# A hybrid SSD / mLSTM / attention kernel: the cells' gate computed feature-major, and ScalarE's squares behind the decays

## The reference, cut to what matters

```python
h = _f32(_rmsnorm(x, ab_norm_g[i]))
proj = h @ _f32(ab_w_in[i])
z_a, xbc, dt_raw, z_b, q, k, v, ig, fg, og = jnp.split(proj, AB_SPLITS, axis=-1)
# _ssd: the state space part
y = y_diag + y_off + xs * d_skip
y = y.reshape(bsz, seqlen, SSD_INNER) * jax.nn.silu(z)              # z_a
yg = _rms(y.reshape(bsz, seqlen, SSD_GROUPS, SSD_INNER // SSD_GROUPS))
return yg.reshape(bsz, seqlen, SSD_INNER) * norm_g
# _mlstm: the matrix-memory cells
h = num / jnp.maximum(jnp.abs(den), jnp.exp(-m_t))[..., None]
h = h * jax.nn.sigmoid(o_raw)
h = _rms(h).reshape(bsz, seqlen, ML_INNER) * norm_g
return h * jax.nn.silu(z)                                            # z_b, the cells' gate
# after both
y = jnp.concatenate([y_a, y_b], axis=-1) @ _f32(ab_w_out[i])
```

## Time and profile before

| | |
|---|---|
| median of three runs | 1588.63 us (1584.34 to 1589.14) |
| the profiled execution | 1582.52 us, span 1580.6 us |
| PE busy / DVE / ACT / POOL, share of the span | 97% / 58% / 41% / 36% |
| mean granted clock of TensorE | 0.992 of 2.4 GHz |
| projection, 80 to 560 us | PE 40.0 us busy in each 40 us |
| scan, 600 to 720 us | PE 36.9 to 37.2 us busy in each 40 us; DVE 35.8 to 36.4 |

### The profile page before, as it was taken

How to read it: one execution, slowest core, us unless ns; L and a number is a source line. 1 busy time by engine, 2 the same in 40 slices (tenths; PEclk the granted TensorE clock), 3 DMA queues, 4 the chain that set the end, 5 groups by cost and what they waited for, 6 DMA issues and landing times.

```text
span 1580.6 us, 23657 instructions
## 1 busy us (share of the span) xinstructions
PE 1527.5 (97%) x9114; PEld 1313.9 (83%) x9114; DVE 911.6 (58%) x1484; ACT 649.0 (41%) x1272; POOL 567.1 (36%) x325
## 2 busy tenths in 40 slices
PE   9999999999999989998999999999999999999897
PEld 8798989898999977776788877888888888787686
DVE  7675878684853459998544263345544235553623
ACT  6542533353432233444345252344555333556421
POOL 3245454545344346566565430132211113211110
PEclk9999999999999989999999999999999999999999
DMA  5132333342334345755585330022111102103612
GB/s 177 41 127 87 123 92 121 93 130 84 121 120 132 116 138 178 225 168 186 180 291 205 121 120 15 14 68 73 61 54 34 34 15 83 63 35 113 253 67 107
DMA packets 151084, 176.42 MB, mean 112 GB/s; under 512 B 9670, under 2 KB 126658, under 8 KB 149954
## 3 DMA queue, kind: packets, MB, share of 16 engines
q1 hardware_dynamic: 150810, 174.92, 34.0%
q10 hardware_dynamic: 168, 0.06, 0.0%
HBM read 122.46 MB, written 52.43 MB: 111 GB/s over the span
## 4 chain that ended last, share of the span: by engine, by line
PE 47%; DVE 2%; issue 1%; DMA 1%; ACT 0%; POOL 0%; SPq 0%; POOLq 0%; DVEq 0%; ACTq 0%
PE b_ps L2404 22%; PE b_ps L2449 4%; PE b_ps L2424 4%; PE b_ps L2354 3%; PE b_ps L2356 3%; PE b_ps L2355 3%; PE b_ps L2436 2%; PE b_ps L2506 2%; PE b_ps L2507 2%; PE b_ps L2508 2%; PE b_ps L2457 1%; PE b_ps L2372 0%; DMA b_yy<-z 0%; DMA z<-b_y_T 0%; DVE b_y_T L2195 0%
## 5 line engine op out<-in xcount | busy, mean ns | idle before, releaser
L1925 POOL TENSOR_TENSOR b_w<-b_w_raw,b_w 128x1024 fp32r<-128x1024 f32 x66 | 158.3, 2399 | 356.0 <-DVE b_w L2184 252.1
L2404 PE MATMUL b_ps<-a_h_hi,b_w 128*128 128x512 f32 x768 | 264.4, 404 | 2.8 <-DVE a_h_lo L2162 2.8
L393 POOL TENSOR_TENSOR b_w<-b_y_T,b_w 128x1024 fp32r<-128x1024 f32 x54 | 141.0, 2614 | 189.7 <-ACT b_w L451 189.7
L2404 PEld LDWEIGHTS b_ps<-a_h_hi,b_w 128*128 128x128 f32 x768 | 144.4, 188 | 36.8 <-issue 3.9
L2404 PE MATMUL b_ps<-a_h_lo,b_w 128*128 128x512 f32 x384 | 150.0, 391 | 0.0
L941 PE MATMUL b_ps<-b_w,p_hi 128*128 128x256 f32 x768 | 139.2, 283 | 0.0
L700 DVE SCALAR_TENSOR_TENSOR b_w_raw<-p_out_raw,p_cols,b_w_raw 128x1024 f32<-128x1024 f32 x60 | 119.8, 2003 | 12.8 <-ACT b_w_raw L482 11.3
L941 PEld LDWEIGHTS b_ps<-b_w,p_hi 128*128 128x128 f32 x768 | 120.1, 192 | 0.6
L941 PE MATMUL b_ps<-b_w,p_lo 128*128 128x256 f32 x384 | 108.7, 283 | 0.0
L2195 DVE CUSTOM_DVE_ANT_0 b_y_T<-b_ps,a_neg_dist 128x128 f32<-128x128 f32 (+5 forms) x96 | 72.1, 777 | 62.8 <-PE b_ps L2424 52.3
L451 ACT CAST b_w<-b_y_T 128x1024 fp32r<-128x1024 f32 x60 | 62.7, 1045 | 106.3 <-DVE b_y_T L661 54.7
(11 more groups left out here) (417 smaller groups left out, 3562.3 us busy)
## 6 DMA issues: line engine op xcount, KB each, us to landing
b_y_T<-in_ab_w_in SPq DMA_DIRECT2D x33, 512.0 KB, 4.4
tok<-p_out_raw SPq DMA_DIRECT2D x64, 256.0 KB, 2.3
b_w_raw<-in_ab_w_out SPq DMA_DIRECT2D x32, 512.0 KB, 3.7
b_w_raw<-in_c_w_in SPq DMA_DIRECT2D x32, 512.0 KB, 4.1
feat<-b_w_raw SPq DMA_DIRECT2D x20, 512.0 KB, 2.7
c_fe<-feat SPq DMA_DIRECT2D x7, 1280.0 KB, 6.7
yt<-b_y_T SPq DMA_DIRECT2D x8, 1024.0 KB, 10.9
b_y_raw<-yt SPq DMA_DIRECT2D x32, 256.0 KB, 4.0
```

The lines of the kernel that those rows point to most:

```text
L393: gp.tensor_tensor(w_lo[s % SLOTS][:, :, :], operand(n, split_of(n, p))[:, :, :], w_hi[s % SLOTS][:, :, :].bitcast(F32), ALU.subtract).the ...
L1925: gp.tensor_tensor(w_lo[:, w, :], w_raw[u % W_RAW][:, :], w_hi[:, w, :].bitcast(F32), ALU.subtract).then_inc(S["l_wlo"], 1)
L2404: mm = pe.matmul(o, x, y, start=(k == 0 and q == 0), stop=(k == KT - 1 and q == 2))
```

## The change

**In the projection** the two z_b blocks are computed feature-major, by the same matmul form as an f block. ACT multiplies each gated area by the norm's gain (one more instruction for each of the 16 areas, behind a wait for the silu), SP stores them into a new DRAM tensor `zt` (8 x 128 x 1024), and a sixth small load brings the gain. `tok` shrinks to 3072 columns.

**In the scan** the cells' norm (without gate and gain) moves from DVE's L1628 to ACT (`memory_norm`), four instructions; the gate multiplies the turned cells' half in the eviction of `turn(n, 0)`, in place of the gain. The gate is loaded by a transfer of its own (`load_gate_cells`), which SP issues behind the store of y and behind a wait for the eviction of `turn(n, 0)`.

**Orders.** ACT: the third group of decays and the cells' weights come before the fourth group, and the squares of y's state space half behind all of them. DVE: `means` behind `s_st`; `turn(n-1, 1)` ahead of the denominator chain; `low_y(0)` moves from chunk 6 to chunk 7. POOL: the power for the cells' mean stands ahead of y plus skip.

```diff
+    gate_turned = lambda n: kinds[n] == "t" and tok_blocks[number[n]][2] is turned_out
...
+                    if gate_turned(n):
+                        sp.dma_start(dest[c0 + 2 * k + b, :, i * BLK:(i + 1) * BLK], area(i, k, b)).then_inc(stored, 16)
...
+                    if gate_turned(n):
+                        gated[0] += 1
+                        nc.scalar.activation(area(i, k, b), area(i, k, b), func).then_inc(S["silu_z"], 1)
+                        act.wait_ge(S["silu_z"], gated[0])
+                        gain = GAIN + c0 + 2 * k + b
+                        nc.scalar.activation(area(i, k, b), area(i, k, b), ACT.Copy, scale=cols[:, gain:gain + 1]
+                                             ).then_inc(S["a_out"], 1)
...
-                    if kinds[n] == "f":
+                    if kinds[n] == "f" or gate_turned(n):
                         fs = slice(b * P, (b + 1) * P)
...
+def load_gate_cells(sp, chunk, n, into, landed):
+    sp.dma_start(into.rearrange("p (f t) -> p f t", t=P), chunk["zt"][:, :, bass.ds(n * P, P)].rearrange("f p t -> p f t")
+                 ).then_inc(landed, 16)
...
                 sp.wait_ge(S["p_cmem"], n + 1)
-                sp.wait_ge(S["d_yb"], n + 1)
                 sp.wait_ge(S["l_yz"], n + 1)
                 load_chunk(sp, chunk, feat, tok, n + 2, par)
                 if behind_first(n):
                     store_y(n - 1, 1 - par)
+                sp.wait_ge(S["d_yT"], n * 4 + 2)
+                load_gate_cells(sp, chunk, n + 2, gz[par][:, 2, :], in_landed[par])
...
-                pe.wait_ge(S["d_yb"] if part == 0 else S["a_ynorm"], (n + 1) * (part + 1))
+                pe.wait_ge(S["a_yb"] if part == 0 else S["a_ynorm"], (n + 1) * (part + 1))
...
+            def memory_norm(n):
+                act.wait_ge(S["l_rstdm"], n + 1)
+                for h in range(ML_HEADS):
+                    yb = y[:, D + h * ML_V:D + (h + 1) * ML_V]
+                    a = nc.scalar.activation(yb, yb, ACT.Copy, scale=rms[:, 2 + h:3 + h])
+                a.then_inc(S["a_yb"], 1)
...
                 memory_squares(n)
-                if isinstance(n, int) and n == TILES - 2:
-                    high_y(0)
-                decays(n + 1, True)
+                memory_norm(n)
+                decays(n + 1, (0, 1, 2))
+                memory_weights(n + 1)
+                decays(n + 1, (3,))
                 ssd_squares(n)
-                decays(n + 1, False)
-                memory_weights(n + 1)
                 ssd_norm(n)
...
+                gp.wait_ge(S["d_meanm"], n + 1)
+                gp.tensor_tensor(rms[:, 2:6], rms[:, 2:6], half[:, 0:4], ALU.pow).then_inc(S["l_rstdm"], 1)
                 gp.wait_ge(S["d_y"], n * 2 + 2)
                 gp.wait_ge(S["l_xd"], n + 1)
                 gp.tensor_tensor(y[:, 0:D], y[:, 0:D], x_tok[:, :], ALU.add).then_inc(S["l_yd"], 1)
-
-                gp.wait_ge(S["d_meanm"], n + 1)
-                gp.tensor_tensor(rms[:, 2:6], rms[:, 2:6], half[:, 0:4], ALU.pow).then_inc(S["l_rstdm"], 1)
...
                 ssd_weights(0)
-                means()
...
                                          op0=ALU.mult, op1=ALU.mult).then_inc(S["d_st"], 1)
 
+                means()
                 dve.wait_ge(S["l_sdec"], n + 0)
...
+                    by = last(gcols[:, 4 * b:4 * b + 4], P) if part else gate_cells(n, par)[:, 4 * b - 8:4 * b - 4, :]
+                    dve.tensor_tensor(y_T[par][:, 4 * b:4 * b + 4, :], b4(i), by, ALU.mult).then_inc(S["d_yT"], 1)
...
+                if behind_first(n):
+                    turn(n - 1, 1, 1 - par)
                 dve.wait_ge(S["p_num"], n * 4 + 4)
...
-                if behind_first(n):
-                    turn(n - 1, 1, 1 - par)
...
-                    if isinstance(n, int) and n == TILES - 2 and k == 0:
+                    if isinstance(n, int) and n == TILES - 1 and k == 0:
                         low_y(0)
...
-                dve.wait_ge(S["l_rstdm"], n + 1)
-                for h in range(ML_HEADS):
-                    v = slice(h * ML_V, (h + 1) * ML_V)
-                    yb = y[:, D + h * ML_V:D + (h + 1) * ML_V]
-                    a = dve.scalar_tensor_tensor(out=yb, in0=yb, scalar=rms[:, 2 + h:3 + h], in1=gates(n, par, 1)[:, v],
-                                                 op0=ALU.mult, op1=ALU.mult)
-                a.then_inc(S["d_yb"], 1)
```

More of the change, by code:

```diff
@@ L145, with projection_ab @@
 T_USED, T_ALL = 56, 64
-def projection_ab(nc, keep, ahead, x, w_in, rows, feat_cols, feat_out, tok_blocks, tok_out, vectors, load_first, chunk):
+def projection_ab(nc, keep, ahead, x, w_in, rows, feat_cols, feat_out, tok_blocks, turned_out, vectors, load_first, chunk):
     nrows = sum(r.shape[0] for r in rows)
@@ L347, in _ @@
                     sp.wait_ge(S["l_wlo"], seq(n, "7") + 1)
-                    for r in (0, 2):
+                    for r in (0, 1, 2, 3):
                         sp.wait_ge(S[f"t_stored{r}"], 16 * (nt - 2))
@@ L1181, in _ @@
             load_chunk(sp, chunk, feat, tok, 1, 1)
+            load_gate_cells(sp, chunk, 1, gz[1][:, 2, :], in_landed[1])
             over(sp, 0, TILES - 2, body)
@@ L1351, in _, with decays @@
         def _(act):
-            def decays(n, first):
-                if first:
+            def decays(n, quads):
+                if quads[0] == 0:
                     act.wait_ge(S["g_ok"], n + 1)
@@ L1359, in decays @@
                     act.wait_ge(S["l_xe"], n + 0)
-                for q in (0, 1) if first else (2, 3):
+                for q in quads:
                     act.wait_ge(S["p_acs"], n * 4 + (q + 1))
@@ L1402, in ssd_norm @@
                                          scale=rms[:, k:k + 1]).then_inc(S["a_ynorm"], 1)
-            decays(0, True)
-            decays(0, False)
+            decays(0, (0, 1, 2))
             memory_weights(0)
+            decays(0, (3,))
             def high_y(u):
@@ L1431, in _ @@
             memory_squares(TILES - 1)
+            memory_norm(TILES - 1)
             high_y(2)
@@ L1558, in turn @@
             def turn(n, part, par, prior=0):
+                if part == 0:
+                    dve.wait_ge(in_landed[par], prior * 48 + 48)
                 if part == 0 and behind_first(prior):
```

58 lines of the change are left out of this document (32 added, 26 removed).

## The result

| | before | after |
|---|---|---|
| median of six runs | 1586.95 us (1584.34 to 1589.14) | 1601.41 us (1600.30 to 1608.45) |
| ratio | | 1.010, 95% interval 1.0081 to 1.0119 |
| the profiled execution | 1582.52, span 1580.6 | 1602.01, span 1600.3 |
| mean granted clock of TensorE | 0.992 | 0.988 |

The changed kernel is 14.5 us slower by the medians, where +4.6 was forecast, and its time is in the range, near the upper end. What follows accounts for the 19.7.

The account below looks back on a forecast made before the run. PE's own work bounds the projection; in the scan PE and DVE hold each other, DVE also held by POOL. Projection -4.1 and scan +8.7 make +4.6 on 1588.6: 1593.2 us, range 1582 to 1603.

Parts of the forecast that it names:

- rival 1: Scan: POOL's sum and its product with the gate both hold DVE's tables; +9.5, so 1602.7 us; chance 0.28.
- The new order up to `num`: Scan chunk: `num` starts at 7.6 for 8.55, the mean at 8.40 for 6.72, `xe` 1.7 later at 13.15.
- The denominator: Scan, DVE: L1577 asks at 13.13 to 13.27, near `xe`'s start; POOL holds the chain, h starts at 15.4 or 17.3.
- the long case: Scan: denominators held by `xe`, then the state's decay; h at 17.3, next chunk after 25.05; taken for chunks 2 to 6.
- the short one: Scan: L1577 passes before `xe`, L1580 is held to its end; h at 15.4, chunk 23.15; chunks 1 and 7.
- The tables: Scan chunk's end: POOL's sum, now behind the power, holds L1065 and PE's decays; next start is h + 7.75.
- The projection: Fourteen products change to f form, 0.32 us less each: -4.5; with +0.4 for the load, -4.1.
- the second copies: Projection, ACT: 16 more instructions delay the weights' cast by some 1.4 us, covered three products ahead; costed at nothing.
- rival 4: The projection gives nothing back, casts late behind second copies or gate loads late; +4 to +5, 1598; chance 0.08.
- The sixth load: Kernel's start: the last small load makes PE wait between 0 and 0.5 us more; taken as +0.4.
- Rival 2: Scan: no denominator is held twice, L1577 asks before `xe` in all chunks; -5.0, 1583.6 us; chance 0.18.
- Rival 3: Scan: DVE's relief reaches PE, whose two idle times go in 7 chunks; up to -8.8, 1573.0 us; chance 0.10.

Follow-up runs that it names:

- the mean early: The changed kernel with ScalarE's squares back behind the second group of decays and DVE's mean back ahead of the eviction into s_qs: 1577.58 us (0.9944).
- undoing the second order: The changed kernel with POOL's sum put back ahead of the power: 1595.67 us (ratio to before 1.0078).
- undoing the first: The changed kernel with the denominator chain put back ahead of the eviction of turn(n-1, 1) on DVE: 1627.32 us (ratio to before 1.0276).

## Why the prediction was right or wrong

**Direction and range: right, the range in part by luck.** Slower was the largest chance (0.45), and the time lies 1.6 inside the upper bound. The value was 8.2 too low, and the difference 9.9 too low, since the median it started from (1588.6, of three runs) lay 1.7 above that of six. The forecast's own bound, all denominators held twice, ends at +7, or 1595.6. The range reached 1603 for the sake of rival 1, which is false; what filled that room was the clock and the casts, which no term of the sum had.

**The new order up to `num`: right.** Mean 8.36 for a forecast of 8.40, `num` 7.75 for 7.6, `xe` at 13.12 for 13.15, `s_e_end` 0.18. One sum in it is wrong as written: 4.8, 1.15, 1.1 and 1.5 make 8.55, not 8.35. In the trace each of ScalarE's groups starts 0.1 to 0.2 ahead of the recorded end of the one before (the last starts are 670.66 and 671.66, the ends before them 670.79 and 671.82), and that overlap, which the text does not name, makes up the 0.2.

**The denominator: right in mechanism, two chunks short.** Held twice, h at 17.31 for 17.3. But chunks 1 to 7 all took the long case; I had 1 and 7 in the short one by a guess that `num` follows sooner there. In chunk 1 it did (7.62 for 7.74), and L1611, at 13.19, still came 0.06 behind `xe`. For chunk 1 that is +1.75, and it was within the bound "all long +7".

**The tables: right in sum, wrong as a price.** h + 7.83 to the next decays for h + 7.75, and L1079 held for 1.94. But the two runs that moved the power alone say that its place cost 0.2 to 0.3 a chunk in the kernel before, and 0.2 to 0.6 here (24.33 and 24.72 to 24.79 for 24.89 to 25.13), since the earlier power feeds the cells' norm. I had it as a loss only.

**The term that was missing: the clock.** PE's idle time ahead of the decays grew from 0.3 to 2.8 us at six starts, which the forecast itself implied (25.05 less the 22 or so of PE's work), and I took all work behind it at full clock. Four half-clock stretches in the scan, 1.7 each, are 6.8 us of the profiled difference. With the one at the start they make 8.5 of the 15.1 us by which the 19.7 exceeds the forecast. (Behind the scan the changed kernel lost 1.3 less to the clock than before, so the whole difference of the two traces in lost clock is 7.3.)

**The projection: two terms mis-sized.** Fourteen products gave 3.4 rather than 4.5: from 200.80 to 396.14, 35 products take 195.34 less 3.06 of waiting, and from 198.65 to 394.38 before 195.73; that is 3.45, or 0.25 each where I took 0.32. And the second copies, "costed at nothing" with "three products ahead" as their cover, cost 3.06 in two places. Together the two are 4.1 us on the forecast: rival 4's mechanism, casts late behind the second copies, and its size (+4 to +5). I had counted the products between a cast and its use, and not what the cast stands behind: in the rows above ScalarE idles 5.75 us for DVE's result, with the cast queued behind the gate that needs it, so each instruction put between them comes straight on top. The sixth load cost 0.5 (first transpose behind it at 8.26 for 7.76), as bounded.

**Rivals.** Rival 1 gives the time almost to the microsecond (1602.7) and is false: L1083 (L1069 before) takes 0.153 to 0.158 in all eight chunks, in the trace's summary of that line. The Trainium skill ("SBUF — State Buffer", "Who interferes with whom": issue order decides) had it pass, and so it did. The hold that the rival feared does exist: in the run with the denominators first, L1081, issued 0.12 behind the product's start, took 2.32. A right number behind a wrong mechanism is luck. Rival 2 is false: L1614's median over the eight chunks is 1.82. Rival 3 was priced as the forecast's opposite, but both are true at once: with the mean early, what is left of the change is worth about 1 us a chunk (22.05 for 23.0), and the late mean hid it. How much of that is DVE's relief and how much the order of the cells' weights (`num` 0.8 earlier) no run separates. I had not asked what the change would be worth with its one bad order left out.

**low_y(0): right in the trace** (-2.8 for -2.7).

## What to carry to other kernels

Follow the last producer of a chain on a third engine before judging a held instruction: here a 0.16 us mean, moved behind squares that nothing needed late, started POOL's `xdt`, `xd` and `xe` 1.7 us later than before, 3.3 later than with the mean early, and cost 24 us. The visible symptoms (denominators, tables) could not be mended one by one: undoing the second order gave back 6 us by the medians, and undoing the first made it 26 us worse, most of it through the clock. Compare chunks with the lost clock taken off before you blame the order for all of a difference. Add to each forecast how long PE will stand in one piece, not only how long in sum. And when a bundle of moves is slower, undo the moves singly, those that look harmless too: one of them may hide a gain of the rest.
